# Keys and values of the latent attention projected in the gate's stage of a two-layer encoder

## What is computed

```python
u = h @ w_in                                   # q_lat 256, kv_lat 128, k_rope 32, gate 1024 columns
q  = rms_norm(q_lat) @ w_qb                    # 16 heads x (64 plain + 32 to be rotated)
kv = rms_norm(kv_lat) @ w_kvb                  # 16 heads x (64 key + 64 value)
s  = q_plain . k_plain + rope(q_pe) . rope(k_rope)
o  = softmax(s) @ v
y  = (o * silu(gate)) @ w_out
```

## Time and profile before

| | us |
|---|---|
| median of three runs | 4001.83 (4000.73 to 4002.47) |
| the profiled execution | 4006.73 |
| its span, first to last instruction | 4004.9 |
| TensorE busy in it | 3780.0 (94%) |
| VectorE, ScalarE, POOL busy | 2355.7 (59%), 2047.8 (51%), 819.1 (20%) |
| gate's stage | 1645.67 to 1852.65 |
| projections of `mla_stage`, to the first scores | 1852.65 to 2054.96 |

### The profile page before, as it was taken

One profiled execution on the slowest core, in us unless ns is written; L12 is line 12 of the kernel. 1 busy time (PEld: TensorE's weight loads), 2 busy tenths in 40 slices (PEclk: granted clock), 3 DMA queues, 4 the chain that ended last, 5 costly groups with the idle time before them and its releaser, 6 DMA issues. The chain is left out here.

```text
span 4004.9 us, 48718 instructions
## 1 busy us (share of the span) xinstructions
PE 3780.0 (94%) x17892; PEld 2991.3 (75%) x17892; DVE 2355.7 (59%) x4235; ACT 2047.8 (51%) x3368; POOL 819.1 (20%) x409
## 2 busy tenths in 40 slices
PE   6999999979998998898889999999999999999799
PEld 3778888868886876686667777777777777777577
DVE  4444443358776555422557777777777777776244
ACT  4333333347765113334456666666666666666521
POOL 0000000011000000002234434444434444444300
PEclk7999999989999998998899999999999999999899
DMA  5453321277663430114821111111111111110243
GB/s 201 145 115 121 106 85 42 62 146 147 124 127 108 132 111 29 66 48 143 249 94 39 39 36 39 36 39 37 39 32 39 37 39 23 37 39 19 78 145 126
DMA packets 297539, 332.22 MB, mean 83 GB/s; under 512 B 153719, under 2 KB 231679, under 8 KB 289943
## 3 DMA queue, kind: packets, MB, share of 16 engines
q1 hardware_dynamic: 283312, 318.59, 28.9%
q10 hardware_dynamic: 13991, 10.52, 1.3%
HBM read 217.10 MB, written 118.62 MB: 84 GB/s over the span
## 5 line engine op out<-in xcount | busy, mean ns | idle before, releaser
L1846 DVE TENSOR_REDUCE ml_peaks<-ml_aux 128x1 f32<-128x512 f32 x1024 | 701.5, 690 | 245.2 <-PE ml_aux L1627 244.7
L1785 ACT ACTIVATE ml_p_f<-ml_scores 128x1024 f32<-128x1024 f32 (+1 forms) x528 | 535.2, 1014 | 574.6 <-PE ml_scores L1627 574.5
L1603 POOL TENSOR_TENSOR ml_p_lo<-ml_p_f,ml_p_hi 128x1024 fp32r<-128x1024 f32 x256 | 615.0, 2402 | 997.8 <-ACT ml_p_hi L1786 983.1
L1786 ACT ACTIVATE ml_p_hi<-ml_scores 128x1024 fp32r<-128x1024 f32 (+1 forms) x528 | 531.2, 1006 | 0.0
L1862 DVE TENSOR_TENSOR ml_p_lo<-ml_p_f,ml_p_hi 128x1024 fp32r<-128x1024 f32 (+1 forms) x272 | 353.4, 1299 | 297.7 <-ACT ml_p_hi L1786 275.3
L1627 PE MATMUL ml_aux<-ml_k_hi,ml_q_hi 96*128 96x512 f32 (+1 forms) x1056 | 416.7, 397 | 16.4 <-DVE ml_peaks L1846 16.2
L1627 PE MATMUL ml_scores<-ml_q_hi,ml_k_hi 97*128 97x512 f32 (+1 forms) x1056 | 416.5, 394 | 7.6 <-DMA ml_q_hi<-ml_peak_rows 7.1
L1627 PE MATMUL ml_out_ps<-ml_p_hi,ml_v_hi 128*128 128x512 f32 x1024 | 407.6, 398 | 15.5 <-POOL ml_p_lo L1603 13.9
L1627 PE MATMUL ml_scores<-ml_q_lo,ml_k_hi 97*128 97x512 f32 (+1 forms) x1056 | 412.7, 391 | 0.0
L1627 PE MATMUL ml_scores<-ml_q_hi,ml_k_lo 97*128 97x512 f32 (+1 forms) x1056 | 409.3, 388 | 0.0
L1627 PE MATMUL ml_out_ps<-ml_p_hi,ml_v_lo 128*64 128x512 f32 x1024 | 403.6, 394 | 0.0
(11 more groups left out here) (220 smaller groups left out, 6955.0 us busy)
## 6 DMA issues: line engine op xcount, KB each, us to landing
o_raw<-mixT SPq DMA_DIRECT2D x36, 512.0 KB, 4.9
late_w<-in_ada_w SPq DMA_DIRECT2D x32, 512.0 KB, 3.7
pr_w_raw<-in_ev_w SPq DMA_DIRECT2D x6, 2048.0 KB, 8.3
x<-o_x SPq DMA_DIRECT2D x18, 512.0 KB, 3.1
v_heads<-hd_result SPq DMA_DIRECT2D x36, 256.0 KB
ml_k_raw<-k_nope SPq DMA_DIRECT2D x16, 576.0 KB, 5.7
ml_q_raw<-q_nope SPq DMA_DIRECT2D x16, 576.0 KB, 7.9
ml_v_raw<-v_heads SPq DMA_DIRECT2D x16, 576.0 KB, 5.3
```

Of the source, the lines that this page charges most:

```text
L1603: nc.gpsimd.tensor_tensor(p_lo[:, u % 3, 0:w], p_f[:, u % 2, 0:w], p_hi[:, u % 3, 0:w].bitcast(FP32), ALU.subtract).then_inc(lo_pool, 1)
L1785: nc.scalar.activation(p_f[:, u % 2, 0:w], src[:, 0:w], ACT.Exp).then_inc(exp_done, 1)
L1786: nc.scalar.activation(p_hi[:, u % 3, 0:w], src[:, 0:w], ACT.Exp).then_inc(exp_done, 1)
L1846: nc.vector.reduce_max(peaks[:, 4 * t + c:4 * t + c + 1], src[:], AX.X).then_inc(peak_done, 1)
```

## The change

`gate_stage` takes the place of `project_stage` for layer 1. It has the same two passes and steps, and from step 4 on each of its 80 steps makes one of 76 further tiles: for each chunk eight key tiles (two heads each) and two value tiles for 128 tokens (eight heads each), three matmuls each, ahead of the step's twelve. VectorE copies such a tile from one of two PSUM banks to one of three slots `heads`, and SP stores it to `k_nope` or `v_heads`. The weights for it (1 MB) are a new input, `mla_w_kv`, loaded behind the gate's weights into the place of `result`; ScalarE and VectorE split them in four parts in the steps 1 to 4, and the latent of a chunk three steps before its first tile. The gate's weights are no longer double: each eighth of the second pass's weights is split as the last chunk of the first pass has used the old one. The gate's banks are six instead of eight, and ScalarE evacuates after the second block of the next chunk instead of the third.

`mla_stage` loads six parts of weights instead of ten, rounds two latents instead of three for a pass, and its list has plain and turned tiles only: 15 in round one, 45 in round two. The keys and values of head 0 are loaded before the first tile is stored, its queries when round one is stored. The keys are split behind the tiles 2 to 6, queries and values behind the tiles 5 to 14 of round two. From the tile 10 of round two on there are two maxima behind a plain tile and one behind a turned one; the list ends with eight behind the last tile. The loads of head 1 come at the tile 18 of round two instead of 24. The semaphores `kept` are shared between the two stages, and `ahead_in` takes the place of one of `local_stage`, with the same waits there.

```diff
+def gate_stage(nc, a, m):
+    RING, KEPT, BANKS = 3, 3, 6
+    FIRST = 4
+    for c, (c0, n) in enumerate(CHUNKS):
+        TILES += [("key", c, j) for j in range(PAIRS)] + [("value", c, f) for f in range(2 * n // P)]
+    for s in range(KT):
+        after.setdefault(s - 1, []).append(("w", 0, s))
+        after.setdefault((NCH - 1) * KT + s + RING, []).append(("w", 1, s))
+    for i in range(4):
+        after.setdefault(1 + i, []).append(("part", i))
+    for c in range(NCH):
+        after.setdefault(FIRST + first_of[c] - 3, []).append(("lat", c))
+    for item in ITEMS:
+        LOWER.append(item)
+        if item[0] == "x" and 0 <= item[1] - 2 - FIRST < len(TILES):
+            LOWER.append(("tile", item[1] - 2 - FIRST))
...
+        def _(sp):
+            sp.dma_start(w_raw[:], passes[0][0]).then_inc(raw_in, 16)
+            sp.dma_start(result[:].rearrange("p f c -> p (f c)"), a["mla_w_kv"]).then_inc(m.ahead_in, 16)
+            sp.wait_ge(lo_done, lo_of["w", 0, KT - 1])
+            sp.dma_start(w_raw[:], passes[1][0]).then_inc(raw_in, 16)
+            for s in range(STEPS):
+                if s >= KT and s % KT == 1:
+                    store(s // KT - 1)
+                if 0 <= s - 1 - FIRST < len(TILES):
+                    keep(s - 1 - FIRST)
...
+        def _(pe):
+            def heads_tile(t):
+                if t >= 2:
+                    pe.wait_ge(lo_done, lo_of["tile", t - 2])
...
+            for s in range(STEPS):
+                pe.wait_ge(lo_done, lo_of["x", s])
+                if 0 <= s - FIRST < len(TILES):
+                    heads_tile(s - FIRST)
+                x_h, x_l = x_hi[:, s % RING, 0:w], x_lo[:, s % RING, 0:w]
+                for f in range(4):
...
+        def _(dve):
+            for item in LOWER:
+                if item[0] == "tile":
+                    dve.wait_ge(step_done, FIRST + t + 1)
+                    if t >= KEPT:
+                        dve.wait_ge(m.kept[t % KEPT], kept_until(t - KEPT))
+                    nc.vector.tensor_copy(heads[:, t % KEPT, 0:tile_cols(t)], heads_ps[t % 2][:, 0:tile_cols(t)]).then_inc(lo_done, 1)
...
 def mla_stage(nc, a, m):
-    PARTS = (2 * QCOLS + 2 * D) // CH
-    PART_ORDER = [0, 3, 2, 5, 6, 8, 1, 4, 7, 9]
+    PARTS = 2 * QCOLS // CH
+    PART_ORDER = [0, 3, 2, 5, 1, 4]
...
             TILES += [("plain", c, 2 * g + i) for g in quads for i in range(2)] + [("turned", c, g) for g in quads]
-            TILES += [("key", c, 2 * g + i) for g in quads for i in range(2)]
-            TILES += [("value", c, 2 * t + (quads[0] > 0)) for t in range(n // P)]
...
-    SPLITS = [t for c in range(NCH) for t in (("k", c), ("q", c))] + [("v", c) for c in range(NCH)]
+    SPLITS = [(kind, c) for kind in "kqv" for c in range(NCH)]
...
     for i in range(NS):
-        SPLIT_TILE.setdefault(FIRST_ROUND + 8 + i // 2, []).append(i)
+        SPLIT_TILE.setdefault(2 + i if i < NCH else FIRST_ROUND + i, []).append(i)
+    at = FIRST_ROUND + 10
     for i in range(NPK):
-        PEAK_TILE.setdefault(min(FIRST_ROUND + 18 + i, len(TILES) - 1), []).append(i)
-    NEXT_LOAD_TILE = FIRST_ROUND + 24
+        if len(PEAK_TILE.get(at, [])) == (1 if TILES[at][0] == "turned" else 2) and at + 1 < len(TILES):
+            at += 1
+        PEAK_TILE.setdefault(at, []).append(i)
+    NEXT_LOAD_TILE = FIRST_ROUND + 18
...
             wave_load(0)
+            load_k(0)
             wave_load(1)
             load_key_rows(0)
+            load_v(0)
             for e in range(len(TILES)):
                 keep(e)
                 if e == FIRST_ROUND - 1:
                     all_kept(e)
-                    load_kq(0)
-                    load_v(0)
+                    sp.wait_ge(kq_in, 16)
+                    load_q(0)
...
-                for r in range(3):
+                for r in range(2):
...
-                if i == 0:
+                if i == 0 and H == 0:
+                    act.wait_ge(kq_in, 16)
+                elif i == 0 or (i, H) == (NCH, 0):
                     act.wait_ge(kq_in, 48 * (H + 1))
...
-                project_stage(nc, a, m, "gt", layer1_passes(a, m))
+                gate_stage(nc, a, m)
```

More of the change, by code:

```diff
@@ L750, in load @@
                 src = m.na_q[pair] if pair < 4 else m.wb_q[pair - 4]
-                for lo, hi, done in ((0, SPLIT, first_qk), (SPLIT, TOK, qk_in[0])) if pair == 0 else ((0, TOK, qk_in[pp]),):
+                for lo, hi, done in ((0, SPLIT, m.ahead_in), (SPLIT, TOK, qk_in[0])) if pair == 0 else ((0, TOK, qk_in[pp]),):
                     for h in range(2):
@@ L1339, in mla_stage @@
     count = lambda kinds, each: np.cumsum([each if t[0] in kinds else 0 for t in TILES]).tolist()
-    by_act, by_dve, by_pool = count(("plain", "key", "value"), 1), count(("turned",), 3), count(("turned",), 1)
+    by_act, by_dve, by_pool = count(("plain",), 1), count(("turned",), 3), count(("turned",), 1)
     group_stores = [16 * sum(2 if TILES[e][0] == "turned" else 1 for e in es) for es in GROUPS]
-    stores_until = lambda g: sum(group_stores[i] for i in range(g % RING, g + 1, RING))
+    stores_until = lambda g: KEPT_BASE + 16 * (g % RING < HEAD_TILES % RING) + sum(group_stores[i] for i in range(g % RING, g + 1, RING))
     def parts_of(e):
         kind, c, f = TILES[e]
[L1346 to L1349, removed]
         return [(r * QCOLS + f * P + (D if kind == "turned" else 0)) // CH for r in range(2)]
     parts_until = [1 + max(PART_ORDER.index(x) for f in range(e + 1) for x in parts_of(f)) for e in range(len(TILES))]
-    SPLITS = [t for c in range(NCH) for t in (("k", c), ("q", c))] + [("v", c) for c in range(NCH)]
+    SPLITS = [(kind, c) for kind in "kqv" for c in range(NCH)]
     NS, NS_KQ = len(SPLITS), 2 * NCH
@@ L1426, in mla_stage @@
         wave_in = [sem(f"wave_in{h}") for h in range(2)]
-        kept = [sem(f"kept{h}") for h in range(RING)]
+        kept = m.kept
         row_in = [sem(f"row_in{h}") for h in range(2)]
@@ L1473, in keep @@
                 sp.wait_ge(act_out, by_act[e])
-                if kind == "value":
-                    sp.dma_start(m.v_heads[c0 // P + f // 2, :, f % 2 * CH:(f % 2 + 1) * CH], place(e)).then_inc(done, 16)
-                else:
-                    dst = m.q_nope if kind == "plain" else m.k_nope
-                    sp.dma_start(dst[f, :, c0:c0 + n], place(e)[:, 0:n]).then_inc(done, 16)
+                sp.dma_start(m.q_nope[f, :, c0:c0 + n], place(e)[:, 0:n]).then_inc(done, 16)
             def all_kept(e):
@@ L1665, in project @@
                 terms = []
-                if kind == "value":
-                    t, half = divmod(f, 2)
-                    (l_h, l_l), (w_h, w_l), n = lat(2), col(2 * QCOLS + D + half * CH, CH), CH
-                    l_h, l_l = l_h[:, t * P:(t + 1) * P], l_l[:, t * P:(t + 1) * P]
-                    terms = [(l_h, w_h), (l_h, w_l), (l_l, w_h)]
-                else:
-                    for r in ((2,) if kind == "key" else (0, 1)):
-                        at = 2 * QCOLS + f * P if kind == "key" else r * QCOLS + f * P + (D if kind == "turned" else 0)
-                        (l_h, l_l), (w_h, w_l) = lat(r), col(at, P)
-                        terms += [(w_h, l_h[:, 0:n]), (w_h, l_l[:, 0:n]), (w_l, l_h[:, 0:n])]
+                for r in range(2):
+                    (l_h, l_l), (w_h, w_l) = lat(r), col(r * QCOLS + f * P + (D if kind == "turned" else 0), P)
+                    terms += [(w_h, l_h[:, 0:n]), (w_h, l_l[:, 0:n]), (w_l, l_h[:, 0:n])]
                 for i, (lhsT, rhs) in enumerate(terms):
@@ L1801, in _ @@
             for e, (kind, c, f) in enumerate(TILES):
-                n = CHUNKS[c][1] if kind != "value" else CH
+                n = CHUNKS[c][1]
                 if e in PASSES and pass_of[e] + 1 < NPASS:
@@ L1949, in build @@
         m.bias_in = ctx.enter_context(nc.semaphore("lc_bias_in0"))
+        m.ahead_in = ctx.enter_context(nc.semaphore("ahead_in"))
+        m.kept = [ctx.enter_context(nc.semaphore(f"heads_kept{i}")) for i in range(3)]
         m.ident = sb("ident_sb", [P, P])
```

157 lines of the change are left out of this document (143 added, 14 removed).

## The result

| | before | after |
|---|---|---|
| median of 20 runs each | 4001.86 us | 4009.05 us |
| ratio after/before (95%) | | 1.0016 (1.0009 to 1.0023) |
| profiled execution, its span | 4006.73, 4004.9 | 4010.9, 4009.1 |
| gate's stage, first load to the next stage's first load | 214.3 (again: 213.1) | 263.9 (again: 263.9) |
| next stage, from there to the first scores | 202.3 (again: 201.4) | 162.8 (again: 159.8) |

What follows compares the result with a forecast made beforehand. TensorE alone bounds the gate stage; in the next stage POOL's chain, the query wait and maxima behind turned tiles waste time. Gate stage +50 and next stage -52 give -2 us: 4000 us, own range 3993 to 4009, 8 in 10 3986 to 4014.

Steps and rivals of the forecast that it cites:

- Gate's stage: Gate stage: 76 added tiles cost TensorE 49.1 us with nothing to hide in; +50.0 us in all (49.1 to 64).
- the 0.4 that I took: Start of gate stage: cost of the 1 MB key and value weight load queued behind the gate weights, 0 to 3.7 us.
- rival 4: Gate stage: slower, new tiles don't fit their steps and short-chunk steps wait for copies, 11 us; 4011 us, chance 0.08.
- From here POOL sets the pace: Round one: POOL's sums and latents take some 6.4 us per chunk against TensorE's 4.1; round two at 1891.
- landing 2: End of round one: the last turned tile's store lands in 2 us, after which head 0's queries can be loaded.
- the 1.5 us for the clock: Round one: two waits of over 2 us lower TensorE's clock, adding 1.5 us to 1889.5 for round two's start.
- From the query load to the end of the first maximum: Round two's start: queries take 7 us from first issue, then VectorE's queue some 10 us; first maximum near 1913.
- From there to the second chunk's turned tile: Round two: from 1913 three plain tiles, half of them at half rate, bring the second chunk's turned tiles to 1922.
- The passes and the tail: Round two: full passes of 22.4 us with today's 6.8 us loss; short chunk's turned tiles at 1986.4, first scores at 2003.
- rival 1: Round two: faster, clock stays up as waits no longer bring half rate, 2.4 us in each of four passes; 3990, chance 0.15.
- rival 3: Round two: slower, plain tiles at half rate throughout, three full passes grow 5.5 us each to about 25; 4017, chance 0.17.
- rival 2: Next stage: faster, slots awaiting stores cause 2 us of each pass's loss and 3 us of round one; 3989, chance 0.15.

Runs made afterwards that it cites:

- again: A second profile of the same kernel, before or changed, taken later with no edit; gate's stage 213.1 and 263.9 us, next stage 201.4 and 159.8 us.
- both_late: Changed kernel with head 0's value load behind its query load and its five key splits moved to round two; ratio to before 1.0003.
- lat_vec: both_late with the lower latents of passes 1 to 5 subtracted on VectorE instead of POOL; 4003.19 us, ratio to before 1.0003.
- q_together: both_late with head 0's five query splits together ahead of round two's first turned tiles; 4005.60 us, ratio to before 1.0003.
- inter: both_late with each turned tile of round two behind its own two plain tiles; 3994.21 us, ratio to before 0.9982.
- k_late: Changed kernel with head 0's five key splits moved from round one to the first five tiles of round two; ratio to before 1.0016.
- v_rows: Changed kernel with the value load's 576 KB read from another matrix, in 128 long pieces instead of 2304 of 256 bytes; ratio to before 1.0014.
- v_twice: Changed kernel with a second load of 1728 pieces of 256 bytes behind the value load; ratio to before 1.0028.

## Why the prediction was wrong

**Gate's stage: right.** +49.6 us in the first pair of profiles and +50.8 in the second, against +50.0. The start (first load to first matmul) grew by 0.4 in the first pair (9.36 to 9.75) and by 0.1 in the second (9.29 to 9.36), so the 0.4 that I took is not told from nothing. TensorE waits 0.2 us for the copies in all, so rival 4 fell.

**Round one and the query load: the step that failed.** "From here POOL sets the pace", with round two at 38.4 and the query load at 42.4. They came at 43.7 and 51.9 (second profile: 40.9 and 49.0). The sum held what the change removes from round one and left out what it puts in: the loads of keys and values of head 0, 1.15 MB ahead of the stores in SP's queue (the rotated key rows stood there before), and five key splits in ScalarE's and VectorE's order. I priced neither. With the value load and the splits moved back together round two starts at 36.8, the query load comes at 44.5, and the ratio falls to 1.0003. A second term was too small, "landing 2": SP waits 5.3 us for the last stores in the changed kernel (1943.46 to 1948.76) and as long in both_late, which is why its query load comes 2 us late although its round two starts early. The trace of before had 4.4 us for the same wait:

```profile
SPq L1482 <- DMA v_heads<-hd_result: 4.4, 1, 4.4
```

That both_late's 36.8 is where my sum without the 1.5 us for the clock had round two (1889.5, so 36.9) does not show that POOL alone sets the pace: lat_vec takes POOL's chain away, and round two still starts at 36.6, held by the tables, for which I had no term. That part of the figure is luck.

**From the query load to the end of the first maximum: 20.9 us, reckoned 18.** VectorE's queue took 13.0 us, not 10: I added it up by the durations of instructions that ran alone. The excess is a value split of 1.48 us (0.38 reckoned), query splits of 4.2 in all (3.1) and 0.9 of waiting for sums. q_together takes 1.7 us of it away by keeping VectorE's splits apart from POOL's sums and latents. The Trainium skill ("SBUF — State Buffer", section Who interferes with whom) says that a VectorE instruction with two inputs in SBUF contends with a POOL instruction that reads SBUF. The rows here agree (1.26 and 1.70 us for the sum, 0.43 and 1.48 for the value split).

**From there to the second chunk's turned tile: 11.2, reckoned 9.** TensorE has four tiles there, three plain ones and the turned one itself; I counted three.

**The passes and the tail: right.** 22.6, 21.4 and 19.5 us from turned tiles to turned tiles, against 22.4, 22.4 and 19.6; 15.3 us from the short chunk's turned tile to the scores, against 16.6. The clock of these three stretches was 0.85, 0.92 and 0.83: it fell in each, so rival 1 fell, and no pass came near 25 us, so rival 3 did. ScalarE waits only 4.7 us for slots, yet the first two passes lost about as much as before (7.0 and 5.8 us, forecast 6.8): rival 2 fell too. I had sized that rival by one row of each wait, and the trace of before has more: ScalarE waited 32.6 us for slots, not 14.5, and TensorE 8.7 us for ScalarE, not 5.0 "in all".

```profile
ACT hd_result L1808 <- DMA k_nope<-hd_result: 12.0, 5, 3.1
...
ACT hd_result L1808 <- DMA q_nope<-hd_result: 3.5, 4, 1.2
ACT hd_result L1808 <- DMA v_heads<-hd_result: 2.6, 4, 1.0
...
PE ml_out_ps L1627 <- ACT hd_result L1808: 3.7, 1, 3.7
```

That the loss comes with three turned tiles in a row was argued in the forecast. inter takes them apart and gets 1.3 to 2.5 us a pass back, all of it clock, while TensorE's 3.4 us of waits stay: the larger part of the loss is not due to their standing together.

Together: 9.47 + 2.86 + 2.21 - 0.84 (passes) - 1.30 (tail) = 12.4 us late at the first scores by the first profile (9.4 by the second; the medians are 9 us above the forecast). The forecast's rivals held no queue of SP.

## What to carry to other kernels

When a load is moved ahead in a queue, price what it passes: not the load's own time, but that of the issues behind it, read from the longest issue of each line next to the median. Where two edits each hold up the same stretch, taking back one can show nothing; take back both before a cause is called absent. And an order that spreads an engine's long tiles between short ones can be worth more than the work that is moved: here 0.2%, where the moved work gives nothing that the runs can tell (no run tried that order in the kernel before).

## What the runs showed of the hardware

- An issue on SP stood 8.2 to 10.6 us behind a load of 2304 pieces of 256 bytes (four profiles of the changed kernel and k_late), and none stood behind as many bytes in 128 pieces (v_rows). 1728 pieces more did not lengthen it (10.8, v_twice).
- Two VectorE subtractions with both inputs in SBUF took 2.37 us beside a POOL sum, 1.41 without; the sum 1.70 to 1.72, and 1.26 to 1.29 beside VectorE products that read PSUM or beside none. A value split took 1.48 us beside POOL's subtraction, 0.43 without.
- Passes with the same matmuls and the same 3.4 us of TensorE's waits had a granted clock of 1.00 (inter, three waits of 1.1) and of 0.85 and 0.92 (changed kernel, one wait of 2.4 and one of 1.0).
